# Gated linear attention on one Trainium2 core: the keys' exponentials made by ScalarE alone, in eight instructions per block, instead of a VectorE subtraction and one wide exponential

## The reference

```python
b = jnp.cumsum(gi, axis=2)                      # running sum of the log decays
rel = b[:, :, :, None, :] - b[:, :, None, :, :]
decay = jnp.where(causal, jnp.exp(jnp.minimum(rel, 0.0)), 0.0)
sc = jnp.einsum('bhid,bhijd,bhjd->bhij', qi, decay, ki)
intra = jnp.einsum('bhij,bhjv->bhiv', sc, vi)
inter = jnp.einsum('bhid,bhdv->bhiv', qi * jnp.exp(b), state)
```

## Time and profile before

| | |
|---|---|
| median of 3 runs | 2097.81 us (2092.47 to 2097.97) |
| the profiled execution: its time | 2095.14 us |
| its span, first to last instruction | 2093.2 us |
| mean granted TensorE clock | 0.976 |
| busy: PE, DVE, ACT | 1994.0, 1088.8, 932.5 us |

### The profile page before, as it was taken

The page is one execution under the profiler, slowest core; times in us unless marked ns, Lnnn a source line. Parts: engine busy times, 40 slices in busy tenths (PEclk is TensorE's granted clock), DMA queues, the critical chain, the costliest instruction groups (busy, mean ns, idle before and its releaser), DMA issues.

```text
span 2093.2 us, 25307 instructions
## 1 busy us (share of the span) xinstructions
PE 1994.0 (95%) x9881; PEld 1488.5 (71%) x9881; DVE 1088.8 (52%) x2023; ACT 932.5 (45%) x1737; POOL 12.6 (1%) x28
## 2 busy tenths in 40 slices
PE   8999889999889999899999999999999999999997
PEld 4876446687447788566788888777666668888885
DVE  5623764632874422657656543442386575565333
ACT  3733664643674233564422322344587543233223
POOL 1000000000000000000000000000000000000000
PEclk8999889999989999999999999999999999999998
DMA  8431432123202433003233333415400123333331
GB/s 287 122 87 51 161 101 81 54 79 91 81 21 81 148 94 86 16 1 116 71 100 92 101 93 94 116 53 125 146 2 1 51 71 101 96 95 98 94 94 48
DMA packets 301268, 183.13 MB, mean 87 GB/s; under 512 B 17551, under 2 KB 292109, under 8 KB 299949
## 3 DMA queue, kind: packets, MB, share of 16 engines
q1 hardware_dynamic: 295437, 166.05, 27.4%
q10 hardware_dynamic: 4704, 13.31, 1.7%
q0 software_dynamic: 1008, 2.15, 0.3%
HBM read 179.22 MB, written 2.27 MB: 87 GB/s over the span
## 4 chain that ended last, share of the span: by engine, by line
PE 84%; DVE 8%; ACT 5%; issue 1%; DMA 1%; another core or an unknown queue 0%; ACTq 0%; DVEq 0%
PE PS L903 22%; PE PS L905 22%; PE PS L904 22%; PE PS L1049 3%; PE PS L1077 2%; PE PS L1062 2%; PE PS L1203 1%; DVE WLO L2080 1%; DVE SE L2154 1%; ACT WHI L1515 1%; PE PS L1226 1%; PE PS L1121 1%; PE PS L1015 1%; DVE X L2047 1%; PE PS L1130 1%
## 5 line engine op out<-in xcount | busy, mean ns | idle before, releaser
L904 PE MATMUL PS<-LO,WHI 128*128 128x512 f32 x1690 | 659.4, 390 | 0.0
L903 PE MATMUL PS<-HI,WHI 128*128 128x512 f32 x1578 | 626.2, 397 | 23.7 <-DVE LO L2053 9.2
L905 PE MATMUL PS<-HI,WLO 128*128 128x512 f32 x1578 | 616.0, 390 | 0.0
L2080 DVE TENSOR_TENSOR WLO<-RING,WHI 128x1024 fp32r<-128x1024 f32 (+3 forms) x271 | 314.3, 1160 | 530.1 <-ACT WHI L1515 529.1
L1515 ACT ACTIVATE WHI<-RING 128x1024 fp32r<-128x1024 f32 (+3 forms) x271 | 272.6, 1007 | 469.0 <-PE PS L905 446.7
L903 PEld LDWEIGHTS PS<-HI,WHI 128*128 128x128 f32 x1578 | 297.2, 188 | 105.7 <-issue 27.1
L904 PEld LDWEIGHTS PS<-LO,WHI 128*128 128x128 f32 x1690 | 318.4, 188 | 65.1 <-issue 1.7
L905 PEld LDWEIGHTS PS<-HI,WLO 128*128 128x128 f32 x1578 | 297.1, 188 | 63.0
L903 PE MATMUL PS<-HIDDEN,WHI 128*128 128x512 f32 x352 | 137.1, 390 | 0.6 <-PE PS L905 0.6
L905 PE MATMUL PS<-HIDDEN,WLO 128*128 128x512 f32 x352 | 137.0, 389 | 0.0
L904 PE MATMUL PS<-HIDDEN,WHI 128*128 128x512 f32 x352 | 136.9, 389 | 0.0
(11 more groups left out here) (333 smaller groups left out, 2302.7 us busy)
## 6 DMA issues: line engine op xcount, KB each, us to landing
RING<-in_ffn_w_up SPq DMA_DIRECT2D x88, 512.0 KB, 3.8
RING<-in_w_in SPq DMA_DIRECT2D x48, 512.0 KB, 3.9
RING<-in_w_mod SPq DMA_DIRECT2D x32, 512.0 KB, 4.1
RING<-in_ffn_w_down SPq DMA_DIRECT2D x32, 512.0 KB, 4.0
RING<-in_ev_w_in SPq DMA_DIRECT2D x30, 512.0 KB, 4.0
RING<-in_w_out SPq DMA_DIRECT2D x16, 512.0 KB, 4.5
RING<-in_od_w_in SPq DMA_DIRECT2D x15, 512.0 KB, 4.0
RING<-in_ffn_w_down SPq DMA_DIRECT2D x16, 384.0 KB, 3.4
```

Of the source, the lines that this page charges most:

```text
L903: mm(bank, WHI[i2][:, i, :], hi, start=(k == 0), stop=False)
L904: mm(bank, WHI[i2][:, i, :], lo, start=False, stop=False)
L905: return mm(bank, WLO[i2][:, i, :], hi, start=False, stop=last)
L2080: tt(WLO[i2][:, 0:nk, :], raw, WHI[i2][:, 0:nk, :], ALU.subtract).then_inc(me.signals(w_split), 1)
```

## The change

ACT computes the keys' exponentials straight from the running sums: for each of the eight reference points one ACTIVATE of 128 columns, exp(bias - b), with the reference column as its bias and -1 as its scale. DVE's L2302, the semaphore `keys_to_exp`, and ACT's wait for it are gone. `keys_exp` is now signalled eight times, and DVE waits for the eighth. Since ACT is now the first to write the buffer, it waits itself for `gla_own` from block 2 on.

```diff
-        keys_to_exp, keys_exp, keys_ready = (sem(n) for n in ("keys_to_exp", "keys_exp", "keys_ready"))
+        keys_exp, keys_ready = sem("keys_exp"), sem("keys_ready")
...
                 def within(qb):
-                    act.wait_ge(keys_to_exp, me.after(keys_to_exp))
-                    fn(GK2[qb % 2], GK2[qb % 2], ACT.Exp).then_inc(me.signals(keys_exp), 1)
+                    if qb >= 2:
+                        act.wait_ge(gla_own, NB * l + qb - 1)
+                    for a in range(8):
+                        fn(GK2[qb % 2][:, a, :], z(BT)[:, qb * B:qb * B + B], ACT.Exp, bias=BREF[:, 8 * qb + a:8 * qb + a + 1], scale=-1.0) \
+                            .then_inc(me.signals(keys_exp), 1)
                     act.wait_ge(gla_to_act, me.after(gla_to_act))
                     fn(GPROD[qb % 2], GPROD[qb % 2], ACT.Exp).then_inc(me.signals(gla_act), 1)
...
                 def exponents(qb):
                     bb = z(BT)[:, qb * B:qb * B + B]
                     dve.wait_ge(*me.last)
-                    tt(GK2[qb % 2], BREF[:, 8 * qb:8 * qb + 8].unsqueeze(2).broadcast_to([P, 8, B]), heads(bb, 8), ALU.subtract) \
-                        .then_inc(me.signals(keys_to_exp), 1)
                     tt(GPROD[qb % 2].rearrange("p c (a j) -> p c a j", a=8), within(bb), over(bb), ALU.subtract) \
                         .then_inc(me.signals(gla_to_act), 1)
...
-                    dve.wait_ge(keys_exp, me.after(keys_exp))
+                    dve.wait_ge(keys_exp, me.after(keys_exp, 8))
                     stt(GK2[qb % 2], GK2[qb % 2], 1.0, heads(z(GK)[:, qb * B:qb * B + B], 8), ALU.min, ALU.mult) \
                         .then_inc(me.signals(keys_ready), 1)
```

## The result

| | before | changed |
|---|---|---|
| median of 20 runs | 2094.5 us | 2101.02 us |
| lowest to highest | 2089.26 to 2100.41 | 2095.18 to 2108.99 |
| span of the profiled execution | 2093.2 us | 2101.5 us |

The ratio is 1.0032 with a 95% interval of 1.0022 to 1.0041: the changed kernel is 6.7 us slower (4.6 to 8.6). The median of before fell from 2097.81 to 2094.5 us as its runs went from three to twenty, so of the distance between the forecast of 2107.0 and the measured 2101.02 about 3.3 us is a better known base, and about 2.5 us an effect that is smaller than the 9.2 us forecast.

The account below looks back on a forecast made before the run. PE waiting for ACT in each "mix" block was taken as the bound. Block delays summed to 9.2 us, taking the profiled 2095.14 to 2104.3; with the median 2.7 us higher, the forecast was 2107.0 us, range 2100 to 2114.

Parts of the forecast that it names:

- What bounds the stage: In "mix" no engine is full; in each block PE waits for ACT before L1130, 0.52 to 2.31 us, and DVE has room.
- ACT is 1.43 us longer in each block: Keys' exponentials on ACT: eight at a pitch of 0.296 us take 2.37 us where one wide took 0.94.
- The time rule with no overlap between instructions: Skill's budget of about 0.3 us per ACTIVATE with bias pointer: about 2.1 us more per block, sum near 13; set aside.
- Where it lands: Delay reaching PE, blocks 0 to 3: layer 0 0.92, 0 (hidden by weight transfers), 1.2, 1.43; layer 1 1.43, 1.35, 1.4, 1.43 us.
- The forecast for PE's waits: PE's idle time before L1130 for ACT grows about 1.4 us in each block except block 1 of layer 0.
- The sum of 9.2 us: Delays of the eight "mix" blocks added up; nothing behind "mix" takes any of it back.
- On the path it gives the 0.40 us of block 0, layer 0, and no more: Removing eight DVE subtractions, at most 9.8 us of DVE time, saves only ACT's 0.40 us wait for DVE there.
- DVE late by 0.9 us at L2314: DVE's L2314 would wait about 0.9 us for the last exponential, where it did not wait before.
- The stated sign of being wrong: Pitch far from 0.30, "mix" growing while a later stage shrinks, or its clock (0.89, 0.91) moving more than a few hundredths.
- DVE was the bound: Rival: the chain runs through DVE's subtraction in each block, so removing it gives up to about 9 us, 2089; chance 0.03.
- Most of it is absorbed: Rival: five of eight blocks swallow the delay, about 4 us remain, 2102, not told from no change; chance 0.19.
- The clock takes more: Rival: longer PE gaps bring two more 5 us stretches at the lower 1.2 GHz level, +14, 2112 us; chance 0.15.

## Why the prediction was right, point by point

*What bounds the stage.* Right for block 0 of each layer, where DVE waits for no exponential and PE's wait for ACT grew, and borne out as a whole: lengthening ACT's turn alone, with the subtraction kept, gives the whole loss (+7.5). In blocks 1 to 3 DVE's wait for the last exponential grows with it, and how much goes by which is open.

*ACT is 1.43 us longer in each block.* Right: 2.33 or 2.34 us against 0.94, so 1.4. The split of that into 0.73 for the operand pointer and 0.66 for the cut was not foreseen. The time rule with no overlap between instructions, which would have made the sum about 13, was rightly set aside: the measured pitch is 0.29.

*Where it lands.* By experiments, 2.9 and 4.8 us in layers 0 and 1 against 3.5 and 5.6. By the profiles of the two kernels with the change in one layer, block by block, 0.97, 0.53, 1.13 and 1.27 in layer 0 (forecast 0.92, 0, 1.2 and 1.43), and 1.27, 1.97, -0.54 and 1.35 in layer 1 (forecast 1.43, 1.35, 1.4 and 1.43). The delay in block 1 of layer 0 was hidden for the most part: between its L1203 matmuls only 0.14 us is left. The forecast for PE's waits, about 1.4 more in each other block, holds for five of the seven (1.38 or 1.39). Block 0 of layer 0 got 2.01, and in block 2 of layer 1 the wait shrank from 1.23 to 0.65, behind the slow stretch of block 1.

*The sum of 9.2 us* was too large: 6.7, interval up to 8.6. The mechanism held and the size was off. The term that stands out is the 1.4 for block 2 of layer 1, which measured -0.54 with a granted clock of 0.91 in place of 0.82. Since one profile on each side can't tell the edit from the clock, this is where the difference showed and not a proof of its cause. The other candidate is "On the path it gives the 0.40 us of block 0, layer 0, and no more", for the removal of the subtraction. Taking it away alone measured -2.9 us, and 2.5 us more gain there would close the gap exactly. But layer 1's blocks gained nothing by it in the profile, doubling it cost only 0.8, and keeping it with the split cost 7.5, not 9 or more. No run settles where the missing 2.5 us are.

*DVE late by 0.9 us at L2314.* It waited 4.6 us in six blocks, about 0.8 each.

*The stated sign of being wrong.* The prediction allowed the clock of the two stretches a few hundredths. It moved by +0.02 and by -0.05, and in the one profiled pair the two stages didn't grow by 3.5 and 5.6 us: layer 0's, from its first L1121 to its last L1130, went from 97.1 to 96.7 us, layer 1's from 88.1 to 94.8. The sum of these is near the forecast, but the shares are not, and it is the runs with one layer changed that bear the shares out. That a single pair came near in the sum is partly luck.

*The rivals.* "DVE was the bound" is excluded by the sign and by the doubled subtraction. "Most of it is absorbed" is not what happened with the change, but it is what happened to the cut without a pointer: 5.3 us on ACT, +0.4 measured. "The clock takes more" did not raise the median of this change above the sum. It was present in the profiled execution, where block 1 of layer 1 is 3.96 us longer at a clock of 0.60. As a mechanism that makes a longer wait cost more than itself it is neither shown nor excluded.

## What to carry to other kernels

Cutting one ScalarE instruction into several to save work on another engine costs the overlap-corrected start of each piece, and here half of that price on ScalarE was the per-partition bias pointer; compare start to next start, not durations. The kernel's price is not in proportion: 0.66 us more in each block cost nothing that could be measured, 1.39 us cost 6.7, and 2.90 us cost 22.6. When an edit frees an instruction from a dependency, the gain is in moving it into an idle stretch, and after that the engine that is late by the next smallest margin has to be moved as well. Before you put a difference between two profiles down to an edit, look at the granted clock of the stretch in both, and at a stretch that the edit doesn't touch.

## What the hardware showed that was not expected

The kernel before had, in its one profiled execution, a clock of 0.89 in layer 0's "mix", and with the change 0.91, though PE's waits for ACT had grown. In layer 1 it went from 0.91 to 0.86. One profile's clock in one stage is therefore not evidence for an edit.

TensorE also fell to its lower level without a long wait. In block 0 of layer 0 before, its longest waits were 0.86 us for DVE and 0.71 us for ACT, it was busy 8.35 of 10 us at the full clock, and the next 13 us, in which it worked without a pause, were at 0.50:

```profile
212.00:222.00 10.00, 8.35 (x64) 3.67 (x62) 8.83 (x22) 7.27 (x19) 0.00 (x0) 1.00 0.56 192
222.00:235.00 13.00, 13.00 (x62) 6.98 (x60) 10.84 (x18) 3.48 (x10) 0.00 (x0) 0.50 0.36 115
```

The Trainium skill, page "TensorE: Matmul & The Clock Gate", section "HAM oscillation — how this bites in real kernels", describes a kernel that restarts at the low clock after each transfer it waits for. This case agrees only in part: waits for ScalarE of 2.09 and of 2.07 us were followed once by four matmuls in 1.10 us and once by four in 0.66.

An exponential of 128 columns takes 0.20 us from start to start with immediate operands and 0.29 us with one pointer. For short instructions the pointer is nearly half of the price again.
